# Expert weight pieces laid out with 8 KB in a row for each partition, in a decoder trunk with two mixture-of-experts stages

## The reference, cut to what matters

```python
D_MODEL, SEQ, N_EXPERTS, EXPERT_HIDDEN = 1024, 512, 16, 512

for e in range(N_EXPERTS):
    hdn = jax.nn.silu(t @ w_gate[e]) * (t @ w_up[e])     # (512,1024)@(1024,512), twice
    y = y + gate[:, e:e + 1] * (hdn @ w_down[e])         # (512,512)@(512,1024)
```

## Time and profile before

| | us |
|---|---|
| median of 3 runs | 2024.05 (2019.95 to 2027.97) |
| span of the profiled execution, first to last instruction | 2023.0 |
| 16 expert rounds of layer 0, in the span | about 867 to 1174 |
| 16 expert rounds of layer 1, in the span | about 1680 to 1987 |

### The profile page before, as it was taken

The page is one execution under the profiler, slowest core; times in us unless marked ns, Lnnn a source line. Parts: engine busy times, 40 slices in busy tenths (PEclk is TensorE's granted clock), DMA queues, the critical chain, the costliest instruction groups (busy, mean ns, idle before and its releaser), DMA issues. The chain is left out here.

```text
span 2023.0 us, 23771 instructions
## 1 busy us (share of the span) xinstructions
PE 1655.6 (82%) x8285; PEld 1312.1 (65%) x8285; DVE 1112.6 (55%) x1314; ACT 946.1 (47%) x1409; POOL 297.2 (15%) x279
## 2 busy tenths in 40 slices
PE   4899967999999357379999929999998537999991
PEld 2365836999999323368877727776786435888871
DVE  4251473454545551458888843344434454888883
ACT  2132233565566200258777732333444124777771
POOL 0000057222331210211111030000000121101101
PEclk8598975799989668589999969999996757999996
DMA  4130100000000511669999842211110075999993
GB/s 131 64 144 21 63 0 11 16 16 16 22 24 16 212 63 28 235 214 392 391 393 393 324 140 94 69 63 42 42 63 1 7 249 182 392 393 393 392 361 146
DMA packets 146856, 314.41 MB, mean 155 GB/s; under 512 B 13232, under 2 KB 14512, under 8 KB 146032
## 3 DMA queue, kind: packets, MB, share of 16 engines
q1 hardware_dynamic: 134416, 267.46, 37.2%
q0 software_dynamic: 7488, 25.24, 3.4%
q10 hardware_dynamic: 4896, 20.97, 2.5%
HBM read 284.22 MB, written 29.43 MB: 155 GB/s over the span
## 5 line engine op out<-in xcount | busy, mean ns | idle before, releaser
L1033 DVE TENSOR_TENSOR moe_wlo<-moe_raw,moe_whi 128x2048 fp32r<-128x2048 f32 x192 | 436.7, 2290 | 89.2 <-ACT moe_whi L1029 88.9
L1029 ACT ACTIVATE moe_whi<-moe_raw 128x2048 fp32r<-128x2048 f32 x192 | 363.5, 1915 | 44.8 <-DMA moe_raw<-in_moe_w_down_dram 21.1
L1040 PE MATMUL all_bank<-moe_whi,moe_xhi 128*128 128x512 f32 x512 | 207.3, 405 | 4.1 <-DVE moe_xlo L1085 4.1
L1042 PE MATMUL all_bank<-moe_whi,moe_xlo 128*128 128x512 f32 x512 | 201.5, 394 | 0.0
L1041 PE MATMUL all_bank<-moe_wlo,moe_xhi 128*128 128x512 f32 x512 | 201.1, 393 | 0.0
L807 PE MATMUL all_bank<-chunks_nq,chunks_t_diag 128*128 128x64 f32 (+1 forms) x768 | 120.8, 308 | 7.6 <-DVE chunks_nq L721 7.6
L807 PEld LDWEIGHTS all_bank<-chunks_nq,chunks_t_diag 128*128 128x128 f32 x768 | 109.0, 219 | 9.7 <-ACT chunks_t_diag L682 6.5
L1040 PEld LDWEIGHTS all_bank<-moe_whi,moe_xhi 128*128 128x128 f32 x512 | 97.4, 190 | 23.5 <-DVE moe_xlo L1085 4.9
L1042 PEld LDWEIGHTS all_bank<-moe_whi,moe_xlo 128*128 128x128 f32 x512 | 97.0, 189 | 20.9
L1041 PEld LDWEIGHTS all_bank<-moe_wlo,moe_xhi 128*128 128x128 f32 x512 | 97.5, 190 | 18.4
L1040 PE MATMUL all_bank<-moe_whi,moe_hhi 128*128 128x512 f32 x256 | 102.3, 400 | 4.4 <-issue 4.4
(11 more groups left out here) (345 smaller groups left out, 3270.9 us busy)
## 6 DMA issues: line engine op xcount, KB each, us to landing
moe_raw<-in_moe_w_gate_dram SPq DMA_DIRECT2D x64, 1024.0 KB, 12.4
moe_raw<-in_moe_w_up_dram SPq DMA_DIRECT2D x64, 1024.0 KB, 13.4
moe_raw<-in_moe_w_down_dram SPq DMA_DIRECT2D x64, 1024.0 KB, 11.9
out_dram<-moe_yo ACTq DMA_DIRECT2D x32, 512.0 KB, 6.3
attn_xhat<-in_w_kv_dram SPq DMA_DIRECT2D x10, 1024.0 KB, 5.1
attn_xhat<-in_attn_w_q_dram SPq DMA_DIRECT2D x6, 1024.0 KB, 5.2
all_h<-in_rwkv_w_v_dram SPq DMA_DIRECT2D x4, 1024.0 KB, 8.5
all_h<-in_rwkv_w_k_dram SPq DMA_DIRECT2D x4, 1024.0 KB, 6.1
```

Of the source, the lines that this page charges most:

```text
L1029: nc.scalar.activation(whi[slot % SPLITS][:, :], raw[slot % 6][:, :], ACT.Copy).then_inc(m["hi_ok"], 1)
L1033: nc.vector.tensor_tensor(wlo[slot % SPLITS][:, :], raw[slot % 6][:, :], whi[slot % SPLITS][:, :].bitcast(fp32), ALU.subtract).then_inc(m[ ...
L1040: nc.tensor.matmul(bank[b][:, :], hi[:, k0 + k, :], wh[:, k, :], start=begin and k == 0, stop=False)
L1042: ins = nc.tensor.matmul(bank[b][:, :], lo[:, k0 + k, :], wh[:, k, :], start=False, stop=end and k == 3)
```

## The change

The loads now give each partition 8 KB that lie in one stretch in memory. A piece of gate or up is still 512 rows, but partition p gets rows 4p to 4p + 3 of it in place of rows p, 128 + p, 256 + p and 384 + p. A piece of down is now 256 whole rows (the upper or lower half of the matrix) in place of half the columns, and partition p gets rows 2p and 2p + 1.

Since block k of a piece of gate or up now holds rows 4p + k, the transposes of the tokens take every fourth column of `xg`, and those of the hidden values every second column of `hid`, so that the operands' rows match. A down piece now feeds both halves of the output: `pe_down` has a loop of its own in which each of two blocks k goes into bank 5 and bank 6, three matmuls each, so there are still 12 matmuls in a piece. Both banks are complete only after the second down piece. So `act_output` 0 now waits for that piece too, and in ACT's order it moves behind the `split_hi` of the next gate 0, to stand right before `act_output` 1.

```diff
             sp.wait_ge(m["split_ok"], n + 1)
             w = io["moe_w_" + kind][layer, bass.ds(e, 1), :, :]
-            w = w[:, :, 512 * half:512 * half + 512] if kind == "down" else w[:, 512 * half:512 * half + 512, :]
-            sp.dma_start(raw[slot % 6][:, :].rearrange("p (k n) -> p k n", k=4),
-                         w.rearrange("a (k p) n -> p (a k) n", p=P)).then_inc(m["raw_in"][slot % 6], 16)
+            rows = 256 if kind == "down" else 512
+            sp.dma_start(raw[slot % 6][:, :], w[:, rows * half:rows * half + rows, :].rearrange("a (p k) n -> p (a k n)", p=P)).then_inc(m["raw_in"][slot % 6], 16)
...
-                ins = nc.tensor.transpose(bank[kt // 4][:, P * (kt % 4):P * (kt % 4) + P], xg[:, P * kt:P * kt + P], g["ident"][:, :])
+                ins = nc.tensor.transpose(bank[kt // 4][:, P * (kt % 4):P * (kt % 4) + P], xg[:, 512 * (kt // 4) + kt % 4:512 * (kt // 4) + 512:4], g["ident"][:, :])
...
-                ins = nc.tensor.transpose(bank[4][:, P * kt:P * kt + P], hid[:, P * kt:P * kt + P], g["ident"][:, :])
+                ins = nc.tensor.transpose(bank[4][:, P * kt:P * kt + P], hid[:, 256 * (kt // 2) + kt % 2:256 * (kt // 2) + 256:2], g["ident"][:, :])
...
-            product(pe, m, n, slot, 5 + half, hhi, hlo, 0, True, True)
+            pe.wait_ge(m["split_ok"], n + 7)
+            wh, wl = (w[slot % SPLITS][:, :].rearrange("p (k n) -> p k n", k=2) for w in (whi, wlo))
+            for k in range(2):
+                kt = 2 * half + k
+                for col in range(2):
+                    out, at = bank[5 + col][:, :], slice(512 * col, 512 * col + 512)
+                    nc.tensor.matmul(out, hhi[:, kt, :], wh[:, k, at], start=kt == 0, stop=False)
+                    nc.tensor.matmul(out, hhi[:, kt, :], wl[:, k, at], start=False, stop=False)
+                    ins = nc.tensor.matmul(out, hlo[:, kt, :], wh[:, k, at], start=False, stop=kt == 3)
+            ins.then_inc(m["piece_used"], 1)
...
                 if not first:
-                    act_output(act, main, e - 1, 0, piece(e, x, 2)[0])
                     hi()
+                    act_output(act, main, e - 1, 0, piece(e, x, 3)[0])
                     act_output(act, main, e - 1, 1, piece(e, x, 3)[0])
                     store_output(act, main, e - 1, (e - 1) * P)
...
             for half in range(2):
-                act_output(act, main, NE - 1, half, piece(NE, 0, half)[0])
+                act_output(act, main, NE - 1, half, piece(NE, 0, 1)[0])
             store_output(act, main, NE - 1, (NE - 1) * P)
```

More of the change, by code:

```diff
@@ L1281, in further_round @@
                     for half in range(2):
-                        act_output(act, more, c, half, c * 6 + (4 + half))
+                        act_output(act, more, c, half, c * 6 + 5)
                     store_output(act, more, c, b * (NE * P) + e * P)
```

## The result

| | us |
|---|---|
| before, median of 4 runs on the same chip | 2022.03 (2019.95 to 2027.97) |
| changed, median of 4 runs | 2036.49 (2032.80 to 2042.83) |
| ratio, with its 95% interval | 1.0075 (1.0051 to 1.0099) |
| span of the profiled execution, before and after | 2023.0 and 2035.0 |

The change makes the kernel slower, by 14.5 us from median to median. The forecast was 2033.1, inside a range from 2018 to 2048. Each run of the changed kernel took 2.2 us longer than its span, as the profiled one did (2037.2 against 2035.0).

A forecast was written before the change was run, and what follows sets the result against it. A closed chain through PE, ACT and DVE bounds most expert rounds, the DMA loads the late ones. 12.7 us for the chain plus 1.0 for the ends, less 4.6 from the loads, make 9.1: 2033.1 us, range 2018 to 2048.

The forecast's parts named there:

- The ring: Expert rounds: closed chain from down 1 through output copy, store, tokens, splits, hidden transposes and products; 18.19 us, forecast 18.68.
- The trial: Late rounds of before: second output copy late by 0.36 us, PE's wait for `hid` longer by 0.34.
- Rivals 1 and 2: Expert rounds: the copy's 0.49 us is absorbed, 2020.4 us, chance 0.20; or a further gain, 2013 us, chance 0.05.
- The second bound: Late expert rounds: loads at 392 GB/s take 18.7 us; 8 KB rows at 415 take 17.7, giving back 4.6 us.
- The copy: Moved first output copy on ACT: 0.49 us more in each of 26 rounds, 12.7 us in all.
- The strided reads: Token and hidden transposes on PE: taken as costing nothing, at most 135 ns each.
- The cover of the tokens: Token transposes on PE: up to 0.77 us more is hidden, since PE would otherwise wait for `hid`.
- Rival 3: Token and hidden transposes: strided reads decide, at most 0.85 us a round, 22 us, 2055 us; chance 0.16 in part or whole.
- The ends: After each layer's last down product: both copies follow it instead of one, 0.49 us each, 0.98 in all.
- The step from span to time: Whole kernel: the median of the runs stands 1.05 us above the profiled span, taking 2032.1 to 2033.1 us.
- the line for slower by 0.5%: Whole kernel: upper limit of no detectable change, 2034.2 us; chance of a slower result 0.44.

The follow-up runs named there:

- e3: The kernel before with only the first output copy moved behind the next split, to wait for the second down product; rounds 18.77 us, median 2036.12 us, ratio 1.0073.
- e4: The changed kernel with both output copies and the store moved behind the split of the next down 0; rounds 18.10 us, median 2015.56 us, ratio 0.9975 to before.
- e5: The kernel before with both output copies and the store moved behind the split of the next down 0; rounds 18.03, then 18.7 us; median 2021.53, ratio 0.9995.
- e9: The kernel before with copies behind the splits and a third of the matmuls left out, 2 KB rows; late rounds 18.7 us, 2006.58 us in one run.
- e1: The kernel before with 8 KB rows for gate and up alone and strided token reads; rounds 18.19 us, median 2018.67 us, ratio 0.9993.
- e2: The changed kernel with both transposes reading adjacent columns again; rounds 18.77 us, median 2035.30 us, ratio 1.0056 to before.

## Why the prediction was right, and where it was off

*What bounds the rounds: right.* The ring, read from waits of 0.28 and 0.62 us, was confirmed from both sides: putting 0.49 us of activation into it lengthened every round (e3), taking the copies out shortened them (e4 against the changed kernel, and e5 in its early rounds against before). The trial that I found in the late rounds of before, 0.36 us of lateness passed on as 0.34, told the right thing. Rivals 1 and 2, which needed slack in the ring, fell with e3.

*The second bound: right.* Late rounds at the DMA engines' pace (e9), gone with 8 KB rows (e1). The rate was taken as 415 GB/s, between 390 and 421; it measured 422, at the upper row and not between. It changed nothing, since every value above 393 leaves the ring as the bound.

*The copy: right mechanism, mis-sized.* 0.49 us was the cost of a second activation in a row; it left out that both now start 0.09 later than the one did, for a reason that stays open. The term measured 0.58 for a round of 18.19, 2.3 us more over 26 rounds.

*The strided reads: wrong at one place.* I took nothing for both groups and kept 135 ns a transpose as the upper end. The cover of the tokens held. The hidden ones cost 0.09 to 0.10 us a round, 2.5 us in all. The step that failed was to put them at nothing although they lie in the ring uncovered and the earlier trace rows allowed 26 ns each, 0.10 us for four. That this is just what was measured is in part luck, since the two rows differ in pace and not in the loads themselves: at a clock of 0.50 the median load of line 559 (a step of four numbers) takes 330 ns and one of line 1424 (adjacent) 334, while at 1.00 each strided load takes 70 ns more, of which the overlap with matmuls hides all but about one in a group. So the warning at the end of the prediction, that the full clock could bring out a cost that the half clock hides, was right. Rival 3 as I priced it (2055 us) was far off, its direction right.

*The rule on memory lines.* By the rows of e2 and the changed kernel, a load costs 70 ns more with a step of 16 bytes and with one of 8 alike (211 and 208 ns against 140). By the Trainium skill, page "SBUF — State Buffer", section "Door 1: The DMA port swizzle (why `[64,N]` ≈ `[32,N]`)", two reads from a line of 16 bytes are enough for the full rate, so the step of 8 bytes should be free. The measurement differs from it and decides: for these loads both steps cost the same.

*The sum.* Forecast for the rounds 8.1 us, measured 13.0: 26 x (18.87 - 18.68) is the 4.9 between. The ends, taken as 1.0, measured 0.96 (twice 0.48). Rounds and ends together are 14.0 us, and the medians differ by 14.5, where I had forecast 9.1. That the time still came out only 3.4 us above the forecast is in part luck: the median of before fell from 2024.05 to 2022.03 with its fourth run, and in the span, 2.9 us above the forecast, the stretches ahead of the rounds happened to be 3.8 us shorter. The step from span to time, taken as 1.05, was 2.2. The forecast lay 1 us below the line for slower by 0.5%, and the two unpriced 0.09s carried it over: I had given that 0.44, and same 0.51.

## What to carry to other kernels

Before a change of layout is made to speed up transfers, ask how far the transfers are what ends the round, and what the new layout does to the order of the rest: here 8 KB rows gave 7.4% more rate and could save 4.6 us of 2022, while the division of the down weights that came with them moved a copy of 0.6 us into the one chain that closes the round, which by itself cost 10.5 us in the rounds. A long chain through several engines that returns to its start is found by following one stall backwards, and a disturbed stretch of the same trace shows whether lateness in it is passed on. When two bounds lie within 3% of each other, price the removal of each alone and of both: here the shorter ring was worth 0.2 us alone, the longer rows 4.6, and both together 6.8.

## What the runs showed of the hardware that I had not expected

- A float32 weight load of 128 x 128 at the full clock takes 140 ns from adjacent columns, 211 ns with a step of four numbers and 208 with a step of two; beside matmuls only some 0.09 us for a group of four or eight transposes is left of it. At half the clock, elsewhere in the kernel before, the median load took 330 ns with a step of four numbers and 334 from adjacent columns.
- Loads from memory in 2 KB rows stop at 392 GB/s with a share of 1.05 of the engines, in 8 KB rows at 422 with 1.02.
- An activation that waits for a product starts either 0.42 to 0.44 or 0.50 to 0.53 us after that product's start. The length of ACT's idle time doesn't sort the two: output copies start after 0.43 with idle times of 0.23, 0.74 and 2.12 us, and after 0.51 or 0.52 with 0.40 and 0.89. What does is open.
